# ScalarE instead of VectorE multiplies the GELU by the gate, and VectorE adds its own rows between two dot products

## The chip, the core and the metric

One core of a Trainium2 chip. The metric is the device time of one execution in microseconds. All numbers are float32. TensorE is called PE here, GpSimd POOL and ScalarE ACT where a row of the profile does so, and VectorE DVE.

## What is computed

Two layers of a trunk, over one block of 128 context tokens (block 0, group "P") and two blocks of 128 latent tokens (blocks 1 and 2, group "S"). Each layer is a token mixer (mLSTM, then attention) and behind it an expert lookup. It is the lookup that the change touches:

```python
def peer_ffn(h, w_q, subkeys, u, v):
    ...
    def one_block(xb):
        ...
        eidx = jnp.take_along_axis(cidx, pos, axis=-1)
        g = jax.nn.softmax(top, axis=-1).astype(xb.dtype)
        act = jax.nn.gelu(jnp.einsum('tped,td->tpe', u[eidx], xb), approximate=False)
        return jnp.einsum('tpe,tped->td', g * act, v[eidx])
```

For each token 8 heads choose 16 experts each, 128 in all. Of each expert a row of `u` (1024 numbers) is dotted with the token, the GELU of that is multiplied by the gate `g`, and the expert's row of `v` is added with this weight.

## The kernel before

**Groups.** There are 6 lookups (2 layers by 3 blocks), each of 128 slots, a slot being one expert for each of the 128 tokens. `u` and `v` lie side by side in memory, so one indirect DMA of POOL (L605) brings a slot: 128 rows of 8 KB, 1 MB. Two slots (GS = 2) are a group, so a lookup has 64 groups and the kernel 384. `rows` holds 12 slots, that is RING = 6 groups.

**The body of a group n on each engine.** VectorE waits for the two slots and makes two dot products (L1136, each with a short read of its accumulator), then raises `dots`. Then it does what is left of group n-1: `weigh` (L1120) multiplies the two GELU columns by two gate columns into `wv`, and raises `weighted`; and, for those groups whose ring place is in SIDE_PLACES (5 of 6 places in the lookups of block 0, 3 of 6 in the others), `add_up` (L1125) adds the second slot's `v` row with its weight into the tile `side`, 1024 columns wide. ScalarE waits for `dots`, makes the GELU of group n (all of ScalarE's activations are on L856) and then, when `weighted` of n-1 is there, the diagonal matrices of group n-1: a copy of the identity scaled by a column of `wv`, one for each slot that PE adds (one where there is a side sum, else two). PE, one group further behind, waits for the diagonals of n-2 and adds diagonal times `v` rows into the PSUM tile `acc` (L674; a diagonal costs two halves of 512 columns, which show as four matmul records). POOL gathers into a ring place anew when `summed` says that PE is done with the group six before, and `side_summed` that VectorE is.

**The order of the work.** `PLAN` is one list of steps for all engines. `spread` cuts the groups of a lookup into runs, ("GROUPS", layer, block, from, to), and puts them between the steps of the trunk by estimated costs; there are 178 runs, most of one or two groups. Every engine goes through the list in order; on ScalarE and VectorE some steps that wait for PE stand one run later (`in_order`). The last lookup has nothing beside it and is one run of 64 groups, a loop over registers. Steps that the text speaks of: PS (an expert choice's scores; VectorE copies them in L1388), PT, PC, PG (VectorE's top 16, ..., the gates; PG ends with the gate columns in L1446), NORM (ScalarE's square of x, VectorE's L1089 behind it), MLA to MLC (the mLSTM; the state product is in MLB, read by L1290), AS (attention scores, read by L1503), MOD (modulation from the weights in_ada_w) and FIN (L1520 adds `acc` and `side` when all 64 groups are summed). `dve_step` counts the steps that VectorE has finished.

**The functions of the change.** On ScalarE `group` and `last_groups`; on VectorE `weigh`, `add_up`, `group` and `last_groups`, which `run_groups` calls.

Of the kernel before, what the change touches and what calls it, by code (L numbers as in the profile page):

```python
# [15 lines left out]
ALU = mybir.AluOpType  # L16
ACT = mybir.ActivationFunctionType
AX = mybir.AxisListType

P = 128  # L20
# [12 lines left out]
SLOTS = PH * TOPK  # L33
GS = 2
GROUPS = SLOTS // GS
QUARTERS = 4
QH = PH // QUARTERS
RING = 6
# [8 lines left out]
BLOCKS = {"P": [0], "S": [1, 2]}  # L47
# [118 lines left out]
PLAN = list(plan())  # L166
# [124 lines left out]
def dve_ends(s):  # L291
    return s[0] in ("MLV", "MLG", "MLB", "MLN", "MLO", "OUT", "PT", "PC", "PG", "AN", "FIN", "YOUT", "NORM") \
        or (s[0] == "MOD" and s[2] in (1, 4))
# [27 lines left out]
def has_side(order, ring):  # L321

    return ring in SIDE_PLACES[order]
# [7 lines left out]
def trunk(nc, A, O):  # L331
    ctx = ExitStack()
    with ctx:
# [15 lines left out]
        gate = sb("gate", [P, 3, SLOTS])  # L349
        act_in = sb("act_in", [P, RING, GS])  # L350
        act_out = sb("act_out", [P, RING, GS])
        wv = sb("wv", [P, RING, GS])
# [34 lines left out]
        xn, at = area(0, D)  # L387
# [3 lines left out]
        cv, at = area(at, KC, 2 * P)  # L391
        va, at = area(at, 2, MH, DV + 1)
        Cst, at = area(at, MH, DV + 1)
# [12 lines left out]
        qkv, at = area(D, 2, QKV)  # L406
        qTa, at = area(at, AH // 2, 2 * P)
        kTa, at = area(at, AKV, 3 * P)
        kdup, at = area(at, AKV, 2, HD)
# [5 lines left out]
        qTp, at = area(D, NSETS, 2 * P)  # L415
        sc, at = area(at, NSETS, NKEYS)
        cand, at = area(at, PH // 2, TOPK * TOPK)
# [39 lines left out]
        act_step, dve_step = sem("act_step"), sem("dve_step")  # L457
# [8 lines left out]
        dots, gelus, weighted, diags, summed = sem("dots"), sem("gelus"), sem("weighted"), sem("diags"), sem("summed")  # L466
# [70 lines left out]

        GORDER = [(0, 0), (0, 1), (0, 2), (1, 0), (1, 1), (1, 2)]

        def run_groups(eng, s, body, last_ones):  # L540

            _, l, b, lo, hi = s
            order = GORDER.index((l, b))
            base = order * GROUPS

            def straight(g0, g1):  # L550
                for g in range(g0, g1):
                    n = base + g
                    body(order, n, g * GS, n % RING, n // RING, g)

            g = lo
            if g < 3:
                straight(g, min(3, hi))
                g = min(3, hi)
            whole = (hi - g) // RING
            if whole >= 2:  # L560
                with eng.Fori(0, whole) as i:
                    for k in range(RING):
                        n = base + g + k
                        body(order, i * RING + n, i * (RING * GS) + (g + k) * GS, n % RING, i + n // RING, None)
                g += whole * RING
            straight(g, hi)
            if hi == GROUPS:
                last_ones(order, base + GROUPS)
# [282 lines left out]
        def _(act):  # L851
# [3 lines left out]
            def f(out, in_, func, **kw):  # L855
                return nc.scalar.activation(out, in_, func, **kw)  # L856
# [13 lines left out]
            def diagonals(order, n, ring):  # L870

                act.wait_ge(weighted, n + 1)
                for j in range(GS - has_side(order, ring)):
                    last = f(diag[:, ring * GS + j, :], ident, ACT.Copy, scale=wv[:, ring, j:j + 1])
                last.then_inc(diags, 1)

            def group(order, n, slot, ring, turn, g):
                act.wait_ge(dots, n + 1)
                f(act_out[:, ring, :], act_in[:, ring, :], ACT.Gelu).then_inc(gelus, 1)
                if g != 0:  # L880
                    diagonals(order, n - 1, (ring - 1) % RING)

            def last_groups(order, n):
                diagonals(order, n - 1, (n - 1) % RING)
# [6 lines left out]
            for n_entry in in_order("A"):  # L891
                s = PLAN[n_entry]
# [11 lines left out]
                if dves:  # L904
                    act.wait_ge(dve_step, dves)
                if k == "GROUPS":
                    run_groups(act, s, group, last_groups)
                    continue
                if noted():
                    act.wait_ge(act_chain, noted())  # L910
# [10 lines left out]
                elif k == "NT":  # L921
                    _, l, w, b = s
# [3 lines left out]
                    place = tok(b - (b > 0))  # L926
                    for q in range(4):
                        last = f(hT[:, q, place], t[:, q * P:(q + 1) * P], ACT.Identity,
                                 scale=gain[:, l, w, q, c:c + 1], bias=modT[:, l, 24 * w + q, c:c + 1])
                    last.then_inc(act_freed, 1)  # L930
                elif k == "MLQK":
                    _, g, half = s
# [3 lines left out]
                elif k == "CONV":  # L936
                    _, g, half = s
# [141 lines left out]
        def _(dve):  # L1079
# [33 lines left out]
                        last.then_inc(dve_chain, one())  # L1113
                last.then_inc(dve_step, 1)

            def weigh(b, n, slot, ring):

                dve.wait_ge(gelus, n + 1)
                g = gate[:, b, slot:slot + GS] if isinstance(slot, int) else gate[:, b, bass.ds(slot, GS)]
                V.tensor_tensor(wv[:, ring, :], act_out[:, ring, :], g, ALU.mult).then_inc(weighted, 1)  # L1120

            def add_up(n, ring):

                dve.wait_ge(weighted, n + 1)
                V.scalar_tensor_tensor(side[:], rows[:, ring * GS + GS - 1, D:2 * D], wv[:, ring, GS - 1:GS], side[:],  # L1125
                                       ALU.mult, ALU.add).then_inc(side_summed, 1)

            def group(b, place):
                def body(order, n, slot, ring, turn, g):
                    if g == 0:  # L1130
                        V.memset(side[:], 0.0).then_inc(side_zero, 1)
                        dve.wait_ge(side_zero, n // GROUPS + 1)
                    for j in range(GS):
                        r = ring * GS + j
                        dve.wait_ge(rows_in[r], turn * 16 + 16)
                        last = V.tensor_tensor_reduce(out=rows[:, r, 0:D], in0=rows[:, r, 0:D], in1=xb[:, place, :],  # L1136
                                                      scale=1.0, scalar=0.0, op0=ALU.mult, op1=ALU.add,
                                                      accum_out=act_in[:, ring, j:j + 1])
                    last.then_inc(dots, 1)
                    if g != 0:  # L1140
                        weigh(b, n - 1, slot - GS, (ring - 1) % RING)
                        if has_side(order, (ring - 1) % RING):
                            add_up(n - 1, (ring - 1) % RING)
                return body

            def last_groups(b):
                def body(order, n):
                    weigh(b, n - 1, SLOTS - GS, (n - 1) % RING)
                    if has_side(order, (n - 1) % RING):
                        add_up(n - 1, (n - 1) % RING)  # L1150
                return body

            V.memset(cs[:], 0.0).then_inc(zeroed, 1)
            dve.wait_ge(inputs_in, 48)
            for n_entry in in_order("D"):
# [14 lines left out]
                if k == "GROUPS":  # L1170
                    if s[3] == 0:

                        dve.wait_ge(experts_chosen, QUARTERS * GORDER.index((s[1], s[2])) + 1)
                    run_groups(dve, s, group(s[2], GORDER.index((s[1], s[2])) % 2), last_groups(s[2]))
                    continue
                if noted():
                    dve.wait_ge(dve_chain, noted())
# [412 lines left out]
```

## Time and profile before

| what | us |
|---|---|
| median of 3 runs (2792.4 to 2797.18) | 2794.21 |
| span of the profiled execution, first to last instruction | 2786.9 |
| what lies around the span: median less span | 7.3 |
| PE busy (71%) | 1975.1 |
| VectorE busy (68%) | 1892.9 |
| POOL busy (31%) | 859.4 |
| ScalarE busy (21%) | 592.2 |
| gathers' packets, share of 16 DMA engines | 71.4% |
| packets of all other DMAs, the same | 17.2% |

The span is of one execution under the profiler; the profile gives no time of its own for that execution beside its span. Matmuls overlap and their ends are modelled. A row of the timeline has start, length, engine, line, operation, what is written from what, and in brackets the engine's idle time before it with who ended it. "x4" merges four instructions that follow each other.

### The profile page before, as it was taken

The numbers are of one execution on the slowest core, as the hardware profiler recorded it, in microseconds if no ns is written. First come the engines' busy times: TensorE is split into PE (matmuls) and PEld (weight loads), VectorE is DVE, ScalarE is ACT, GpSimd is POOL, SyncE is SP. The second block draws the span as 40 slices with busy tenths as digits, with TensorE's granted clock in tenths as the row PEclk, the third lists the DMA queues.
The fourth block names the chain that finished last, engine by engine and source line by source line (L and its number), as shares of the span: only waits on it lengthen the run. The fifth ranks groups of instructions, "written<-read, shape, count | busy, mean of one in ns | idle before, by whom it ended". The sixth has DMA issues, their size and how long they took to land. (4 is left out here: it accounts for less than half of the span.)

```text
span 2786.9 us, 22939 instructions
## 1 busy us (share of the span) xinstructions
PE 1975.1 (71%) x6742; PEld 1141.2 (41%) x6742; DVE 1892.9 (68%) x4473; ACT 592.2 (21%) x1595; POOL 859.4 (31%) x772
## 2 busy tenths in 40 slices
PE   6775686697777665677776775778868765767665
PEld 5465364365433222343443353445634322322222
DVE  1326885776877993256669765767778799866665
ACT  1211223332111211113212121232211121211111
POOL 0001322223333341123334423222343333444442
PEclk9787897799788887688888888677989877888888
DMA  9975797599898998899999988766999998899997
GB/s 340 308 200 226 290 363 289 219 355 356 355 376 362 382 390 315 305 362 395 352 358 415 412 319 336 277 245 246 381 371 408 367 402 362 361 391 422 422 422 293
DMA packets 259304, 958.06 MB, mean 344 GB/s; under 512 B 19700, under 2 KB 156916, under 8 KB 160884
## 3 DMA queue, kind: packets, MB, share of 16 engines
q0 software_dynamic: 110592, 805.36, 71.4%
q1 hardware_dynamic: 141296, 147.00, 16.6%
q10 hardware_dynamic: 7300, 4.33, 0.5%
q8 instruction: 52, 0.85, 0.1%
q14 instruction: 64, 0.52, 0.0%
HBM read 953.74 MB, written 2.89 MB: 343 GB/s over the span
## 5 line engine op out<-in xcount | busy, mean ns | idle before, releaser
L674 PE MATMUL acc<-rows,diag 128*128 128x512 f32 x2136 | 1182.8, 706 | 480.1 <-ACT diag L856 473.4
L605 POOL DMA_INDIRECT rows<-in_uv,eidx x768 | 859.2, 1119 | 1888.8 <-PE acc L674 1307.0
L1136 DVE CUSTOM_DVE_ANT_0 rows<-rows,xb 128x1024 f32<-128x1024 f32 x768 | 916.4, 1221 | 252.1 <-DMA rows<-in_uv,eidx 251.8
L674 PEld LDWEIGHTS acc<-rows,diag 128*128 128x128 f32 x2136 | 461.4, 226 | 1126.4 <-ACT diag L856 618.3
L856 ACT ACTIVATE act_out<-act_in 128x2 f32<-128x2 f32 x384 | 78.0, 203 | 1539.4 <-DVE act_in L1136 1538.8
L1125 DVE SCALAR_TENSOR_TENSOR side<-rows,wv,side 128x1024 f32<-128x1024 f32 x234 | 300.6, 1284 | 8.3
L623 PE MATMUL bank<-wt,hT 128*128 128x256 f32 x896 | 202.0, 386 | 11.4 <-ACT hT L856 7.4
L856 ACT ACT_TABLE_LOAD x137 | 175.8, 1283 | 138.8 <-DVE st L1089 36.7
L623 PE MATMUL bank<-hT,wt 128*128 128x256 f32 (+1 forms) x960 | 183.6, 353 | 17.9 <-DMA wt<-in_peer_w_q 12.6
L856 ACT ACTIVATE diag<-small,wv 128x128 f32<-128x128 f32 x534 | 192.0, 387 | 0.1
L623 PEld LDWEIGHTS bank<-wt,hT 128*128 128x128 f32 x896 | 173.2, 194 | 45.3 <-ACT hT L856 9.4
L623 PEld LDWEIGHTS bank<-hT,wt 128*128 128x128 f32 x960 | 164.3, 198 | 45.0 <-DMA wt<-in_peer_w_q 12.8
L623 PE MATMUL bank<-arena 128*128 128x64 f32 (+4 forms) x480 | 114.2, 429 | 14.3 <-DVE arena L1326 12.3
L623 PEld LDWEIGHTS bank<-arena 128*128 128x128 f32 (+1 forms) x480 | 95.1, 275 | 43.7 <-issue 17.7
L640 PE MATMUL bank<-small,arena 128*128 128x128 f32 x208 | 38.4, 340 | 81.2 <-DVE arena L1196 27.5
L1184 DVE TENSOR_TENSOR modT<-bank,small 128x4 f32<-128x4 f32 x48 | 7.3, 161 | 129.0 <-PE bank L623 128.9
L623 PE MATMUL bank<-wt,cs 128*32 128x256 f32 x432 | 37.1, 485 | 61.0 <-DMA wt<-in_ada_w 60.8
L1120 DVE TENSOR_TENSOR wv<-act_out,gate 128x2 f32<-128x2 f32 x384 | 60.2, 157 | 27.3 <-ACT act_out L856 27.3
L856 ACT ACTIVATE arena<-bank 128x256 f32<-128x256 f32 (+2 forms) x126 | 42.8, 372 | 152.4 <-PE bank L623 119.5
L640 PE MATMUL bank<-small,hT 128*128 128x128 f32 x160 | 37.9, 378 | 48.1 <-ACT hT L856 48.1
L640 PEld LDWEIGHTS bank<-small,arena 128*128 128x128 f32 x208 | 30.5, 175 | 96.6 <-issue 56.6
L1388 DVE COPY arena<-bank 128x512 f32<-128x512 f32 x24 | 16.5, 687 | 69.3 <-PE bank L623 68.8
(154 smaller groups left out, 1362.3 us busy)
## 6 DMA issues: line engine op xcount, KB each, us to landing
wt<-in_ada_w SPq DMA_DIRECT2D x27, 1024.0 KB
wt<-in_peer_w_q SPq DMA_DIRECT2D x26, 1024.0 KB
rows<-in_ada_w SPq DMA_DIRECT2D x21, 1024.0 KB, 12.0
wt<-in_mlstm_w_in SPq DMA_DIRECT2D x14, 1024.0 KB
rows<-in_uv,eidx POOLq DMA_INDIRECT x768
wt<-in_attn_w_qkv SPq DMA_DIRECT2D x12, 1024.0 KB
rows<-in_mlstm_w_in SPq DMA_DIRECT2D x10, 1024.0 KB, 12.1
wt<-in_attn_w_out SPq DMA_DIRECT2D x8, 1024.0 KB
```

Source lines behind the costliest of these rows:

```text
L605: nc.gpsimd.indirect_dma_start(out=rows[:, r, :], out_offset=None, in_=A["uv"], in_offset=bass.IndirectOffsetOnAxis(ap=eidx[:, b, slot:slo ...
L623: return nc.tensor.matmul(out, lhsT, rhs, start=start, stop=stop)
L640: last = nc.tensor.transpose(out[:, i * P:(i + 1) * P], a, ident)
L674: last = nc.tensor.matmul(acc[:, h * 512:(h + 1) * 512], diag[:, r, :], rows[:, r, D + h * 512:D + (h + 1) * 512], start=first and j == 0, ...
L856: return nc.scalar.activation(out, in_, func, **kw)
L1120: V.tensor_tensor(wv[:, ring, :], act_out[:, ring, :], g, ALU.mult).then_inc(weighted, 1)
L1125: V.scalar_tensor_tensor(side[:], rows[:, ring * GS + GS - 1, D:2 * D], wv[:, ring, GS - 1:GS], side[:], ALU.mult, ALU.add).then_inc(side_ ...
L1136: last = V.tensor_tensor_reduce(out=rows[:, r, 0:D], in0=rows[:, r, 0:D], in1=xb[:, place, :], scale=1.0, scalar=0.0, op0=ALU.mult, op1=AL ...
L1184: V.tensor_tensor(modT[:, l, n, :], t[:, 0:4].rearrange("p (n c) -> p n c", c=2), bc(ada_b[:, l, n], 2), ALU.add).then_inc(dve_freed, 1)
L1388: V.tensor_copy(sc[:, n, :], tile(0)[:].rearrange("p (e n) -> p e n", n=NKEYS)).then_inc(dve_freed, 1)
```

## The change

ScalarE waits for its own GELU and multiplies each of its two columns by the gate's column: two copies of one column each, scaled by a column of `gate`, written to `wv`. It raises `weighted` for group n itself, one body earlier than VectorE did, and goes on to the diagonals of n-1. Before each run it also waits until VectorE has made the gates that the run reads (`gates_after`). VectorE has no `weigh` any more. Its side sum of group n-1 stands behind the first of the two dot products of group n, and so ahead of the second; it waits there for `weighted` of n-1, and for its own `dots` of n-1. `dots` of n is raised behind the second dot product as before.

```diff
+        def gates_after(l, b, quarter):
+
+            g = "P" if b == 0 else "S"
+            at = PLAN.index(("PG", l, g, BLOCKS[g].index(b), quarter))
+            return sum(dve_ends(s) for s in PLAN[:at + 1])
...
-            def group(order, n, slot, ring, turn, g):
-                act.wait_ge(dots, n + 1)
-                f(act_out[:, ring, :], act_in[:, ring, :], ACT.Gelu).then_inc(gelus, 1)
-                if g != 0:
-                    diagonals(order, n - 1, (ring - 1) % RING)
+            def gate_at(b, slot):
+                return gate[:, b, slot:slot + 1] if isinstance(slot, int) else gate[:, b, bass.ds(slot, 1)]
+
+            def group(b):
+                def body(order, n, slot, ring, turn, g):
+                    act.wait_ge(dots, n + 1)
+                    f(act_out[:, ring, :], act_in[:, ring, :], ACT.Gelu).then_inc(gelus, 1)
+                    act.wait_ge(gelus, n + 1)
+                    for j in range(GS):
+                        last = f(wv[:, ring, j:j + 1], act_out[:, ring, j:j + 1], ACT.Copy, scale=gate_at(b, slot + j))
+                    last.then_inc(weighted, 1)
+                    if g != 0:
+                        diagonals(order, n - 1, (ring - 1) % RING)
+                return body
...
-                    run_groups(act, s, group, last_groups)
+                    act.wait_ge(dve_step, gates_after(*s[1:3], (s[4] - 1) * QUARTERS // GROUPS))
+                    run_groups(act, s, group(s[2]), last_groups)
...
-            def weigh(b, n, slot, ring):
-
-                dve.wait_ge(gelus, n + 1)
-                g = gate[:, b, slot:slot + GS] if isinstance(slot, int) else gate[:, b, bass.ds(slot, GS)]
-                V.tensor_tensor(wv[:, ring, :], act_out[:, ring, :], g, ALU.mult).then_inc(weighted, 1)
-
             def add_up(n, ring):
 
+                dve.wait_ge(dots, n + 1)
                 dve.wait_ge(weighted, n + 1)
                 V.scalar_tensor_tensor(side[:], rows[:, ring * GS + GS - 1, D:2 * D], wv[:, ring, GS - 1:GS], side[:],
                                        ALU.mult, ALU.add).then_inc(side_summed, 1)
...
                                                       accum_out=act_in[:, ring, j:j + 1])
+                        if g != 0 and j == 0 and has_side(order, (ring - 1) % RING):
+                            add_up(n - 1, (ring - 1) % RING)
                     last.then_inc(dots, 1)
-                    if g != 0:
-                        weigh(b, n - 1, slot - GS, (ring - 1) % RING)
-                        if has_side(order, (ring - 1) % RING):
-                            add_up(n - 1, (ring - 1) % RING)
                 return body
 
-            def last_groups(b):
-                def body(order, n):
-                    weigh(b, n - 1, SLOTS - GS, (n - 1) % RING)
-                    if has_side(order, (n - 1) % RING):
-                        add_up(n - 1, (n - 1) % RING)
-                return body
+            def last_groups(order, n):
+                if has_side(order, (n - 1) % RING):
+                    add_up(n - 1, (n - 1) % RING)
```

## Rows read from the trace of the kernel before

**Rows 1.** The page: busy time, share and instructions of each engine.

```profile
PE 1975.1 (71%) x6742; PEld 1141.2 (41%) x6742; DVE 1892.9 (68%) x4473; ACT 592.2 (21%) x1595; POOL 859.4 (31%) x772
```

**Rows 2.** Stretches: length, busy PE, PEld, DVE, ACT, POOL; clock, DMA share, GB/s.

```profile
2460.00:2760.00 300.00, 208.56 (x377) 83.31 (x376) 194.19 (x341) 42.24 (x157) 133.19 (x116) 0.84 1.00 415
910.00:1050.00 140.00, 86.48 (x183) 35.45 (x181) 134.35 (x401) 27.18 (x72) 53.46 (x48) 0.82 0.97 386
...
436.00:600.00 164.00, 114.19 (x357) 72.78 (x358) 123.81 (x238) 51.00 (x111) 41.09 (x36) 0.81 0.70 263
```

**Rows 3.** Who waited for whom over the span: us in total, times, longest.

```profile
POOL rows L605 <- PE acc L674: 1307.0, 212, 25.8
...
PE acc L674 <- ACT diag L856: 473.4, 154, 23.7
...
DVE rows L1136 <- DMA rows<-in_uv,eidx: 251.8, 162, 11.0
...
POOL rows L605 <- DVE side L1125: 69.1, 13, 15.3
DVE arena L1388 <- PE bank L623: 68.8, 13, 14.4
...
DVE wv L1120 <- ACT act_out L856: 27.3, 12, 14.7
```

**Rows 4.** Groups of instructions: busy us, mean ns, idle before and releaser.

```profile
L856 ACT ACTIVATE diag<-small,wv 128x128 f32<-128x128 f32 x534 | 192.0, 387 | 0.1
...
L856 ACT ACTIVATE act_out<-act_in 128x2 f32<-128x2 f32 x384 | 78.0, 203 | 1539.4 <-DVE act_in L1136 1538.8 <-issue 0.4
...
L1120 DVE TENSOR_TENSOR wv<-act_out,gate 128x2 f32<-128x2 f32 x384 | 60.2, 157 | 27.3 <-ACT act_out L856 27.3
...
L856 ACT ACTIVATE arena<-x 128x1024 f32<-128x1024 f32 x13 | 13.7, 1055 | 86.1 <-DVE x L1524 45.0 <-DVE x L1381 21.9 <-PE bank L623 15.2
```

**Rows 5.** Timeline of VectorE, two bodies between attention steps: start us, length us.

```profile
1868.42 1.22 DVE L1136 CUSTOM_DVE_ANT_0 rows<-rows,xb 128x1024 f32<-128x1024 f32 x1
...
1869.56 1.22 DVE L1136 CUSTOM_DVE_ANT_0 rows<-rows,xb 128x1024 f32<-128x1024 f32 x1
...
1870.71 0.15 DVE L1120 TENSOR_TENSOR wv<-act_out,gate 128x2 f32<-128x2 f32 x1
...
1870.90 1.28 DVE L1125 SCALAR_TENSOR_TENSOR side<-rows,wv,side 128x1024 f32<-128x1024 f32 x1
...
1872.10 1.22 DVE L1136 CUSTOM_DVE_ANT_0 rows<-rows,xb 128x1024 f32<-128x1024 f32 x1
...
1874.39 0.15 DVE L1120 TENSOR_TENSOR wv<-act_out,gate 128x2 f32<-128x2 f32 x1
1874.46 0.55 DVE L1503 TENSOR_REDUCE st<-bank 128x1 f32<-128x384 f32 x1
```

**Rows 6.** Timeline, the first run's end and a norm.

```profile
280.16 0.39 ACT L856 ACTIVATE diag<-small,wv 128x128 f32<-128x128 f32 x1
...
281.72 0.15 DVE L1089 TENSOR_SCALAR st<-st 128x1 f32<-128x1 f32 x1 [0.31 <-ACT xb L856]
```

**Rows 7.** Timeline: PE's links with diagonals ahead, and VectorE's wait for scores.

```profile
511.32 0.29 PEld L674 LDWEIGHTS acc<-rows,diag 128*128 128x128 f32 x1 [0.72 <-ACT diag L856]
...
1440.12 3.33 PE L674 MATMUL acc<-rows,diag 128*128 128x512 f32 x4 [4.10 <-ACT diag L856]
...
1457.11 0.69 DVE L1388 COPY arena<-bank 128x512 f32<-128x512 f32 x1 [4.09 <-PE bank L623]
```

**Rows 8.** Timeline of the last body and the end of the last lookup.

```profile
2767.54 0.20 ACT L856 ACTIVATE act_out<-act_in 128x2 f32<-128x2 f32 x1 [4.45 <-DVE act_in L1136]
2767.65 0.97 ACT L856 ACTIVATE diag<-small,wv 128x128 f32<-128x128 f32 x3
2767.77 0.16 DVE L1120 TENSOR_TENSOR wv<-act_out,gate 128x2 f32<-128x2 f32 x1 [0.20 <-ACT act_out L856]
...
2775.71 1.23 DVE L1520 TENSOR_TENSOR arena<-acc,side 128x1024 f32<-128x1024 f32 x1 [6.46 <-PE acc L674]
```

More of the change, by code:

```diff
@@ L1126, in add_up, with group @@
                                        ALU.mult, ALU.add).then_inc(side_summed, 1)
-            def group(b, place):
+            def group(place):
                 def body(order, n, slot, ring, turn, g):
@@ L1173, in _ @@
                         dve.wait_ge(experts_chosen, QUARTERS * GORDER.index((s[1], s[2])) + 1)
-                    run_groups(dve, s, group(s[2], GORDER.index((s[1], s[2])) % 2), last_groups(s[2]))
+                    run_groups(dve, s, group(GORDER.index((s[1], s[2])) % 2), last_groups)
                     continue
```

## The prediction

> **What bounds the kernel now.** I read the page's busy shares first [rows 1]: no engine is full (PE 71%, VectorE 68%), so no engine alone sets the span. Then the stretches [rows 2], where the reader is to see that the limit changes along the span. In the last block, 2460 to 2760, DMA is at 1.00 and 415 GB/s while VectorE has 194 of 300 us: a transfer bound. In 910 to 1050 VectorE is busy 134.35 of 140 us: a VectorE bound. In 436 to 600 DMA falls to 0.70 and no engine is full: there the trunk's steps and the gather groups take turns, and latency is the bound. So the change must be priced by stretch.
>
> The waits [rows 3] say which wait ends last. VectorE waits 251.8 us for rows. GpSimd waits 1307 us for PE's sums and only 69 us for side sums: a slot comes free when PE is done, and PE waits 473 us for the diagonals that ScalarE makes. VectorE itself waits for PE at the head of trunk steps, 13 times for scores (L1388, 68.8 us) and 6 times at the end of a block (L1520). What a faster VectorE gains ahead of such a wait is lost in it.
>
> **What VectorE sheds.** 384 products of 157 ns, 60 us in all [rows 4]. On the path each costs less or more, by its neighbours' starts [rows 5]. With a side sum: dot to dot 1.14, dot to product 1.15, product to side 0.19, side to dot 1.20, together 3.68 us (the row's columns are start and length); without the product 1.14+1.20+1.15 = 3.49, so 0.19 saved. Without a side sum the product costs the 0.07 between it and the next operation. A body of group n adds the side sum of n-1. Outside the last block I count 203 bodies with and 117 without: 38.6+8.2 = 46.8 us, the ceiling of the gain. In the last block, 31 and 33 bodies, the waits for rows cover it: nothing. Going back from the end along the waits, 77 bodies with and 42 without lie on the path outside it: 14.6+2.9 = **17.5 us saved**.
>
> **What the new order costs.** The sum of n-1 moves ahead of dot 1 of n. The dots of n, which release the GELU, the diagonals of n-1 and then PE, end 1.20 us later in a body with a side sum. The next body's start hardly moves. The side sum ends some 1.3 us earlier, but GpSimd's slot waits are PE's 19 to 1 [rows 3], so I give it nothing; the bounds are 0 and those 69 us, and I take 0, since a slot that opens early only helps where DMA has room.
>
> **What ScalarE takes on.** 768 copies and a wait for its own GELU. No one-column copy with a column scale is in the trace. Its duration: the diagonal of 128 columns takes 387 ns with such a scale; the square of 1024 takes 1055 and the GELU of two 203 [rows 4], thus 0.83 ns a column, and 387 less 106 is an estimated 281 ns. Three diagonals take 0.97 together [rows 8], 0.29 for each further one, so they overlap by 0.09 and copies follow at 0.19. The GELU starts the first diagonal 0.11 after its own start; a waiting product began 0.03 after its end [rows 8]. Afterwards: first copy at 0.20+0.03, diagonal at 0.23+0.19+0.19 = 0.61: **0.50 us later**. Bounds: copies at the GELU's spacing 0.11 give 0.34, at the diagonals' 0.29 give 0.70. I take 0.50, since its terms are from the same form.
>
> The Trainium skill (ScalarE: Activation LUTs, Rules for kernel authors) speaks against the move: multiplications belong on VectorE. By that rule the move is a loss on every group: the 157 ns given up for two copies of an estimated 279 ns each (What ACT_TABLE_LOAD costs: 186 and 93 for a pointer operand), which over 384 groups would be 154 us if ScalarE were the bound. The rows disagree as to the size: ScalarE is idle 1539 us before its GELUs [rows 4], so it has the room, and only the latency counts in my sum.
>
> ScalarE is in order, so behind the copies stand its diagonals and then the trunk step. Three rows show who is waiting.
> - A norm behind a body with a side sum [rows 6]: the diagonal starts at 280.16, the norm's square follows it at once, and VectorE waits 0.31 for that at 281.72. Afterwards the square is 1.20+0.50 = 1.70 later.
> - PE [rows 7]: the sum at 1440.12 waited 4.10 for a diagonal; behind it, with no idle time, come the queries' product, more sums and the scores, for which VectorE waits 4.09 at 1457.11. All of it moves by 1.70.
> - End of a block [rows 8]: diagonals at 2767.65, then PE's sums, for which VectorE idles 6.46. The last side sum isn't ahead of these dots: 0.50.
>
> Along the same path I find ScalarE's diagonals as a link in 9 places behind a body with a side sum and 22 without; 280.16 is the first and 2767.65 the last. One and two of them stand shortly before long waits for rows (up to 11.0 us [rows 3]) that take them in. 8 x 1.70 + 20 x 0.50 = **23.6 us lost**. Two runs of two groups ahead of a state product (448 and 508) become links: there PE already waited 0.72 for the second diagonal [rows 7], which now comes 1.70 later, less the 0.38 that two bodies save and some 0.2 of slack: 1.1 each, **2.2 lost**.
>
> **Edits that cost nothing.** The new wait of ScalarE for gates at each of 178 runs: VectorE makes those gates ahead of the dots for which ScalarE waits anyway; without that cover it would be 2.3 us of dots per run. VectorE's new wait for its weights stands before dot 1: queued behind are that dot and all later VectorE work. The weights are ready 0.04+0.61 us after the dots, the first dot of the next group takes 1.14, so it waits for nothing unless ScalarE is late. It was late for 27.3 us in all, 25 of it in the modulation steps [rows 3], where PE and ScalarE wait for the loads of in_ada_w: taking VectorE's stall away brings those no sooner. Registers for the gate's column are needed in the last block's loop alone, under the rows' waits. No DMA is added or moved in a queue.
>
> **Sum.** -17.5 + 23.6 + 2.2 = +8.3 us. The profiled execution has a span of 2786.9; the runs shown are 2792.4 to 2797.2, so some 7 us lie around the span. On the median of 2794.2 that makes **2802.5 us**.
>
> **Rivals.**
> - VectorE is the bound and the diagonals' delay is hidden. For it: 134 of 140 us in 910 to 1050, and PE's 6 us of slack in many choice steps. Against: the waits at L1388. Time: the 17.5 alone, 2777, at the very most 2747.5 by the ceiling; the case spans 2775 to 2788. It decides where fewer than about 10 diagonals are links. Chance 0.17.
> - A draw: transfers hold the pace. DMA is at 0.97 and 1.00 in two of the stretches [rows 2], and what shifts between such stretches is taken up by waits for rows. Both sums shrink to a third: 2797, or 2789 to 2799. Chance 0.30.
> - The slots starve: PE waits become slot waits. GpSimd waited 212 times for PE; were a quarter of these true links, 53 x 0.50 = 26 us would come on top: about 2829. Against it: where DMA is full, as in the last block, a slot that opens 0.5 later costs nothing. Chance 0.07.
> - The copies need a table load each time: 1283 ns. The diagonals are the same function and stand behind the GELU with no load [rows 8]; chance nearly nil.
> The forecast (2797 to 2815) has 0.46.
>
> **Numbers.** A measurement of this kernel tells about 0.2% (5.6 us) from no change. The forecast case is slower by that with 0.41 and within it with 0.05; the draw is within it with 0.26, else slower 0.03 and faster 0.01; the first rival faster with 0.16. Slower 0.51, same 0.32, faster 0.17. The range reaches from 2785, leaving out most of the first rival, to 2820, which is the forecast at 0.70 us a diagonal (+6) and some 10 us for links that the shift creates.
>
> **What would show it.** ScalarE busy up by 215 us, L1120 gone, copies near 0.28; gelu to diagonal 0.6; side sum between the dots, body 3.49; VectorE's waits at L1388, L1089 and L1520 longer, and longer PE waits for diagonals. It is wrong if VectorE's waits for PE and ScalarE stay and the choice stretches shrink, or if GpSimd's waits for PE grow by more than 50 us with lower DMA shares.

## The result, and the profile after

The changed kernel takes 2865.36 us (median; 2861.17 to 2868.22), the kernel before 2795.69 us beside it (2792.4 to 2801.11): a ratio of 1.0251, interval 1.0221 to 1.0281, so some 70 us slower. The forecast was 2802.5 with a range of 2785 to 2820; the sign was right, the size was outside the range. The profiled execution has a span of 2861.9 us, 75.0 more than the one before. In every run for which both are given, the time is 1.8 to 1.9 us above the run's own span. So the profiled execution of the kernel before took some 2789 us, about 5 us less than its median; the 7 us that were put "around the span" are mostly that.

Busy times of the kernel after, to be read against [rows 1]:

```profile
PE 1994.5 (70%) x6742; PEld 1150.0 (40%) x6742; DVE 1850.2 (65%) x4089; ACT 774.4 (27%) x2363; POOL 862.1 (30%) x772
```

The exchange of work is as announced: VectorE is busy 42.7 us less, ScalarE 182.2 us more (the pair of copies shows 0.48 us, since the two overlap). No engine became full. So the loss is in waits.

The same stretches of the kernel after as in [rows 2] (length, busy PE, PEld, DVE, ACT, POOL; clock, DMA share, GB/s):

```profile
2460.00:2760.00 300.00, 206.64 (x405) 86.19 (x404) 195.82 (x304) 79.67 (x284) 124.19 (x117) 0.84 0.99 409
910.00:1050.00 140.00, 88.40 (x179) 38.12 (x178) 130.93 (x372) 37.37 (x117) 57.61 (x48) 0.79 0.96 384
436.00:600.00 164.00, 104.23 (x320) 65.49 (x320) 109.15 (x203) 54.58 (x131) 35.87 (x33) 0.75 0.65 243
```

The stretches are by the clock on the wall, so they hold slightly other work than before; what counts is their kind. The transfer-bound one keeps its pace (0.99, 409 GB/s). The one bound by latency has DMA at 0.65 instead of 0.70, and VectorE and PE both do less in it.

Waits over the span of the kernel after (us in total, times, longest), against [rows 3]:

```profile
POOL rows L611 <- PE acc L680: 1428.5, 217, 26.3
ACT act_out L862 <- DVE act_in L1147: 1091.5, 279, 16.2
...
PE acc L680 <- ACT diag L862: 538.7, 147, 26.7
...
ACT L862 <- DVE act_in L1147: 378.6, 59, 16.4
DVE rows L1147 <- DMA rows<-in_uv,eidx: 258.1, 154, 12.9
...
DVE side L1136 <- ACT wv L862: 59.2, 41, 16.8
```

PE's waits for diagonals grew by 65.3 us and GpSimd's waits for PE by 121.5. The row that explains them has no tile's name: `ACT L862 <- DVE act_in`, 59 times. It is an instruction that names no tile and starts when the dots are done. The groups of instructions say which (busy us, mean ns, idle before and releasers):

```profile
L862 ACT ACT_TABLE_LOAD x137 | 175.8, 1283 | 474.0 <-DVE act_in L1147 378.6 <-DVE st L1105 32.9 <-DVE st L1511 22.7
L862 ACT ACTIVATE wv<-act_out,gate 128x1 f32<-128x1 f32 x768 | 184.2, 286 | 19.1
```

In the kernel before the same row reads:

```profile
L856 ACT ACT_TABLE_LOAD x137 | 175.8, 1283 | 138.8 <-DVE st L1089 36.7 <-DVE st L1277 23.9 <-DVE st L1505 19.4
```

There are as many table loads as before, 137, and each is as long, 1283 ns. They only stand elsewhere in time: 59 of them now come behind the dots. One of the 59, with 16.4 us, stands there before too, so 58 are new. The two timelines show one and the same place, an attention step followed by the body of group 221 (start, length, idle before and releaser). Before:

```profile
1836.98 1.28 ACT L856 ACT_TABLE_LOAD   x1
...
1844.20 3.23 PE L674 MATMUL acc<-rows,diag 128*128 128x512 f32 x4
...
1847.14 0.08 DVE L1136 DVE_READ_ACCUMULATOR2_ANT act_in<- 128x1 f32 x1
...
1847.26 0.20 ACT L856 ACTIVATE act_out<-act_in 128x2 f32<-128x2 f32 x1 [9.00 <-DVE act_in L1136]
...
1847.81 1.98 PE L674 MATMUL acc<-rows,diag 128*128 128x512 f32 x4 [0.38 <-ACT diag L856]
```

After:

```profile
1901.44 1.22 DVE L1147 CUSTOM_DVE_ANT_0 rows<-rows,xb 128x1024 f32<-128x1024 f32 x1
...
1902.58 1.28 DVE L1136 SCALAR_TENSOR_TENSOR side<-rows,wv,side 128x1024 f32<-128x1024 f32 x1
...
1903.78 1.22 DVE L1147 CUSTOM_DVE_ANT_0 rows<-rows,xb 128x1024 f32<-128x1024 f32 x1
...
1905.08 1.28 ACT L862 ACT_TABLE_LOAD   x1 [11.23 <-DVE act_in L1147]
...
1906.38 0.20 ACT L862 ACTIVATE act_out<-act_in 128x2 f32<-128x2 f32 x1
1906.61 0.48 ACT L862 ACTIVATE wv<-act_out,gate 128x1 f32<-128x1 f32 x2
1907.00 0.39 ACT L862 ACTIVATE diag<-small,wv 128x128 f32<-128x128 f32 x1
1907.20 1.28 DVE L1136 SCALAR_TENSOR_TENSOR side<-rows,wv,side 128x1024 f32<-128x1024 f32 x1 [1.05 <-ACT wv L862]
...
1907.44 1.55 PE L680 MATMUL acc<-rows,diag 128*128 128x512 f32 x2 [2.93 <-ACT diag L862]
```

Before, ScalarE loads the GELU's table right behind its last exponential at 1836.98 and then waits 9.00 us for the dots; the load is free. After, it sits idle for 11.23 us, until the dots are done, and only then loads, 1.28 us. The GELU, the copies, the diagonal, PE's sum and VectorE's next side sum, which waits 1.05 us, are all late by that. (PE's wait for the diagonal, 0.38 us before and 2.93 after, also holds the 1.20 us of the new order and the 0.50 us of the copies.)

Why it stands there is read in ScalarE's instructions at this place in order, with the semaphore that each waits for. Before:

```
L856 ACT_TABLE_LOAD
L856 ACTIVATE act_out<-act_in 128x2 [waits dots]
```

After:

```
L888 semaphore instruction [waits dots]
L862 ACT_TABLE_LOAD
L862 ACTIVATE act_out<-act_in 128x2 [waits dve_step]
```

The source puts the new wait for the gates (`dve_step`) ahead of the GELU's own wait for `dots`. With one wait, it rides on the GELU and the load ahead of it is free to run. With two, one becomes an instruction of its own, ahead of the load, and here it is `dots`, the one that ends last. Of the 62 loads ahead of a group's GELU, 59 stand behind such an instruction for `dots` after, and one before. Whether the two waits in the other order in the source would leave `dots` on the GELU was not tried.

### The profile page after: what moved, and what is told of

It reads as the page before. It is cut to its first block and busy times, and to the rows that moved or that the text cites. A ratio compares the mean times of both kernels' runs of the same rounds, so it can differ in the third digit from the quotient of the medians.

```text
span 2861.9 us, 23732 instructions
## 1 busy us (share of the span) xinstructions
PE 1994.5 (70%) x6742; PEld 1150.0 (40%) x6742; DVE 1850.2 (65%) x4089; ACT 774.4 (27%) x2363; POOL 862.1 (30%) x772
## 5 line engine op out<-in xcount | busy, mean ns | idle before, releaser
L680 PE MATMUL acc<-rows,diag 128*128 128x512 f32 x2136 | 1205.6, 718 | 552.3 <-ACT diag L862 538.7
L680 PEld LDWEIGHTS acc<-rows,diag 128*128 128x128 f32 x2136 | 469.4, 230 | 1205.6 <-ACT diag L862 674.3
L862 ACT ACTIVATE act_out<-act_in 128x2 f32<-128x2 f32 x384 | 78.0, 203 | 1093.7 <-DVE act_in L1147 1091.5
L1136 DVE SCALAR_TENSOR_TENSOR side<-rows,wv,side 128x1024 f32<-128x1024 f32 x234 | 300.2, 1283 | 59.2 <-ACT wv L862 59.2
L862 ACT ACT_TABLE_LOAD x137 | 175.8, 1283 | 474.0 <-DVE act_in L1147 378.6
L862 ACT ACTIVATE diag<-small,wv 128x128 f32<-128x128 f32 x534 | 191.4, 386 | 0.0
L862 ACT ACTIVATE wv<-act_out,gate 128x1 f32<-128x1 f32 x768 | 184.2, 286 | 19.1
L629 PE MATMUL bank<-hT,wt 128*128 128x256 f32 (+1 forms) x960 | 182.2, 352 | 6.0 <-ACT hT L862 6.0
L629 PE MATMUL bank<-arena 128*128 128x64 f32 (+4 forms) x480 | 112.9, 427 | 17.5 <-DVE arena L1332 13.6
L862 ACT ACTIVATE arena<-bank 128x256 f32<-128x256 f32 (+2 forms) x126 | 42.7, 370 | 153.5 <-PE bank L629 114.1
L646 PEld LDWEIGHTS bank<-small,arena 128*128 128x128 f32 x208 | 29.8, 172 | 97.3 <-issue 59.5
```

The source lines that it names most:

```text
L629: return nc.tensor.matmul(out, lhsT, rhs, start=start, stop=stop)
L646: last = nc.tensor.transpose(out[:, i * P:(i + 1) * P], a, ident)
L680: last = nc.tensor.matmul(acc[:, h * 512:(h + 1) * 512], diag[:, r, :], rows[:, r, D + h * 512:D + (h + 1) * 512], start=first and j == 0, ...
```

## The experiments

The theory tested, L: the second wait holds some 59 loads behind the dots, and this is most of the loss. Its rivals: O, the new order and the later diagonals starve the slots; C, the copies themselves load ScalarE too heavily. Every ratio below is to the kernel before, with five rounds; 1% is 28 us.

**The wait moved.** In the changed kernel:

```diff
-                    act.wait_ge(dve_step, gates_after(...))
...
                     f(act_out[:, ring, :], act_in[:, ring, :], ACT.Gelu).then_inc(gelus, 1)
+                    if g == first:
+                        act.wait_ge(dve_step, gates)
                     act.wait_ge(gelus, n + 1)
```

> The changed kernel, with ScalarE's new wait for the gates moved from ahead of a run of groups to behind the first GELU of the run, ahead of its two copies. Theory L (the load): with two waits ahead of the first GELU, the load of the GELU's table (1.28 us) comes behind the dots in 59 of 178 runs instead of beside them, and this is most of the loss. Then this kernel has the ACT_TABLE_LOAD waiting for dots at most a few times, its time falls by 50 to 65 us to about 2800 to 2815, and ScalarE's table loads wait about 139 us in all as in [rows 4]'s kernel. Theory O (the order): the side sum between the dots and the 0.5 us later diagonals cost it, starving the slots; the time stays at 2855 to 2865 and GpSimd's waits for PE stay at about 1430 us.

Measured: 1.0085 (1.0058 to 1.0111), 24 us above the kernel before, where the change has 70. The wait in its place cost 46 us (35 to 58 by the two intervals), somewhat under the expected 50 to 65. Its table loads:

```profile
L862 ACT ACT_TABLE_LOAD x137 | 175.8, 1283 | 114.1 <-DVE st L1107 29.6 <-DVE st L1285 20.3 <-DVE act_in L1149 16.4
```

16.4 us of waits for dots are left, one place, and that one the kernel before has too. GpSimd's waits for PE are at 1358.4 us, not at the 1430 of theory O. Rival C asked for 2850 us or more and falls here too: all 768 copies are in this kernel, and it is at 1.0085.

**The wait alone.** The kernel before, and nothing but this:

```diff
                 if k == "GROUPS":
+                    act.wait_ge(dve_step, gates_after(...))
                     run_groups(act, s, group, last_groups)
```

> The kernel before, with nothing changed but the wait of ScalarE for the gates ahead of each of its 178 runs of groups; the wait is redundant there, since VectorE does the product with the gate itself. Theory L: 59 or so table loads come behind the dots, 1.28 us each, up to 75 us; the time rises by 45 to 75 us to 2840 to 2870. Theory O: the wait is always met in time, so no change, 2795 within 6 us.

Measured: 1.0129 (1.0106 to 1.0152), 36 us slower by a wait that is always met in time. This is somewhat under the expected 45 to 75. The loads are behind the dots again:

```profile
L862 ACT ACT_TABLE_LOAD x137 | 175.8, 1283 | 465.8 <-DVE act_in L1143 342.8 <-DVE st L1096 35.7 <-DVE st L1512 27.3
```

Theory O has no place for this result.

**The wait kept, the load moved ahead of it.** In the changed kernel:

```diff
+                    f(spare[:], ident[:, 0:1], ACT.Gelu)
                     act.wait_ge(dve_step, gates_after(...))
```

> The changed kernel, both waits left ahead of each run's first GELU, but a one-column GELU of the identity into a spare tile put ahead of them: it waits for nothing of the run, so a table load can be made there, before the waits. Theory L (the wait costs only because it leaves the 1.28 us load behind the dots): as wait_behind_gelu, 2805 to 2825, with no table load that waits for dots. A rival W (a second wait ahead of the GELU is itself dear, for the semaphore or ScalarE's sequencer): it stays near 2850 to 2865.

Measured: 1.0075 (1.0051 to 1.0098), 21 us. Both waits stand where the change has them, 178 GELUs are added, and 49 us come back. No load waits for dots any more:

```profile
L863 ACT ACT_TABLE_LOAD x137 | 175.8, 1283 | 95.4 <-DVE st L1107 33.5 <-DVE st L1285 20.2 <-DVE st L1513 14.9
```

The wait as such is therefore not dear (rival W falls); what it does to the load is.

**The order alone.** The kernel before, with the product and the side sum of the group before placed between the two dots:

```diff
+                        if g != 0 and j == 0:
+                            weigh(b, n - 1, slot - GS, (ring - 1) % RING)
+                            if has_side(order, (ring - 1) % RING):
+                                add_up(n - 1, (ring - 1) % RING)
                     last.then_inc(dots, 1)
-                    if g != 0:
...
```

> The kernel before, with VectorE's product and side sum of the group before placed between the two dot products; ScalarE as it was. Theory L with the terms of the prediction: dots of a body with a side sum end 1.2 us later (and 0.2 for the product), 8 links of 1.4 us plus about 20 of 0.2, so 10 to 20 us slower, 2805 to 2815. Theory O: most of the 70 us appears, 2840 or more.

Measured: 1.0073 (1.0046 to 1.0101), 20 us: at the upper end of what L says, far from the 44 and more of O.

**The order taken back.**

```diff
-                        if g != 0 and j == 0 and has_side(order, (ring - 1) % RING):
-                            add_up(n - 1, (ring - 1) % RING)
                     last.then_inc(dots, 1)
+                    if g != 0 and has_side(order, (ring - 1) % RING):
+                        dve.wait_ge(dots, n + 1)
+                        add_up(n - 1, (ring - 1) % RING)
```

> As wait_behind_gelu, but with the side sum back behind both dot products, so that only the copies on ScalarE are left of the change. Theory L: 17.5 us saved on VectorE, 28 links of 0.5 us lost, about 2790 to 2800, 8 to 12 us below wait_behind_gelu. Theory O: near the kernel before as well if the order is what costs, but then 50 us or more below wait_behind_gelu. A third theory C (the copies themselves load ScalarE too heavily ahead of its diagonals): 2850 or more here and in wait_behind_gelu, and no change in the two kernels made from the kernel before.

Measured: 1.0048 (1.0029 to 1.0066), 13 us. Against wait_behind_gelu the order is worth 10 us (1 to 19 by the two intervals). It was to be near nothing against the kernel before, and isn't: either the copies cost more than 14 us or the dropped product brings less than 17.5. Two kernels tell these apart.

**The copies alone.**

```diff
                 f(act_out[:, ring, :], act_in[:, ring, :], ACT.Gelu).then_inc(gelus, 1)
+                act.wait_ge(gelus, n + 1)
+                for j in range(GS):
+                    f(spare[:, ring, j:j + 1], act_out[:, ring, j:j + 1], ACT.Copy, scale=act_in[:, ring, j:j + 1])
```

> The kernel before with the wait for the own GELU and two scaled one-column copies added behind it, into a spare tile; VectorE keeps its product and its order. It measures the delay alone. The prediction's term: the diagonals 0.5 us later at 28 links, +14 us, 2800 to 2810. If the change's saving on VectorE (17.5 us) is real, this kernel is some 17 us slower than wait_behind_old_order, about 2820 to 2825; if the saving is hidden, it equals it at about 2805.

Measured: 1.0052 (1.0032 to 1.0071), 14.5 us, the expected 14.

**The product alone taken away.**

```diff
-                V.tensor_tensor(wv[:, ring, :], act_out[:, ring, :], g, ALU.mult).then_inc(weighted, 1)
...
-                    last = f(diag[:, ring * GS + j, :], ident, ACT.Copy, scale=wv[:, ring, j:j + 1])
+                    last = f(diag[:, ring * GS + j, :], ident, ACT.Copy, scale=act_out[:, ring, j:j + 1])
```

> The kernel before without VectorE's product: the multiplication of GELU by the gate is left out of the computation, and the diagonals and the side sum take the GELU itself. It measures what the dropped product is worth. The prediction's term: 17.5 us faster. wait_behind_old_order (product dropped, copies added) and before_two_copies (copies added, product kept) stood at +0.48 and +0.52%, so by those two the saving is near nothing: 0 to 6 us faster.

Measured: 0.9977 (0.9961 to 0.9993), 6.4 us faster, 2 to 11 by the interval. The other pair that differs by the product, before_two_copies and wait_behind_old_order, is 1 us apart. Three rows of its trace:

```profile
PE 1977.6 (71%) x6742; PEld 1141.1 (41%) x6742; DVE 1863.1 (67%) x4089; ACT 591.6 (21%) x1595; POOL 869.6 (31%) x772
```

```profile
POOL rows L605 <- PE acc L674: 1317.0, 206, 25.8
...
DVE rows L1134 <- DMA rows<-in_uv,eidx: 283.1, 179, 11.3
```

VectorE is busy 29.8 us less than before and waits 31.3 us more for rows. GpSimd's wait for PE, which sets when rows are asked for, has hardly moved. That fits a VectorE that became free and waits for the same rows. It isn't shown: the execution in this trace is the longest of the 12 (a span of 2796.3 us, 9.4 above the one of the kernel before), and the same row in before_two_copies, which keeps the product, is 257.3 us, in wait_behind_old_order 268.6.

**The diagonals in their own body.** The kernel before has to make the diagonals of a group one body late, since VectorE makes the weights there. The change lifts this bond and doesn't use it. With the wait behind the GELU, and in the new order:

```diff
                     last.then_inc(weighted, 1)
-                    if g != 0:
-                        diagonals(order, n - 1, (ring - 1) % RING)
+                    diagonals(order, n, ring)
                 return body
...
             def last_groups(order, n):
-                diagonals(order, n - 1, (n - 1) % RING)
+                pass
```

> wait_behind_gelu with the three diagonals (two or one per group) of a group made in its own body, right behind its copies, instead of in the next body. In the kernel before they had to wait for VectorE's product of the next body; now ScalarE has the weights itself. Theory D (PE waits for diagonals only because they are made one body, often one run, too late): PE's waits for diagonals fall from 508 us to below 350, slots come free sooner, and the time falls below the kernel before, to 2700 to 2780. Rival: the sums' order and the slots hold the pace, PE then waits for the next group's diagonals as long; 2800 to 2815, as wait_behind_gelu.

Measured: 0.9802 (0.9774 to 0.9830), 55 us faster than the kernel before and 79 faster than wait_behind_gelu, from which it differs by this alone; the rival falls. PE's waits for diagonals fall to 376.8 us, less far than theory D's 350. Then the side sum was put back behind both dots, by the edit of wait_behind_old_order:

> own_body_new_order with the side sum back behind both dot products. If the order's cost (10 us between wait_behind_gelu and wait_behind_old_order) stands here too, 0.2 to 0.5% below own_body_new_order: ratio 0.975 to 0.978. If the side sum is now what frees the slots (GpSimd waits 200.7 us for it in own_body_new_order, against 69.1 in the kernel before), a later side sum costs: 0.980 to 0.985.

Measured: 0.9792 (0.9770 to 0.9814), median 2736.35 us, 58 us faster. The two own-body kernels can't be told apart by these intervals; the order's 10 us don't show here. Waits of own_body_old_order:

```profile
POOL rows L611 <- PE acc L680: 976.4, 161, 26.4
...
PE acc L680 <- ACT diag L862: 368.4, 112, 17.7
POOL rows L611 <- DVE side L1136: 367.9, 78, 19.0
```

PE waits 105 us less for diagonals than in [rows 3], and GpSimd 331 us less for PE. The side sum is now what frees many slots (367.9 us against 69.1 in [rows 3]), so the order's two effects, earlier side sums and later dots, may cancel; that was not tried further. The timeline of the same kernel at group 221, the place of the timelines above, shows what is gained:

```profile
1812.23 7.63 PE L680 MATMUL acc<-rows,diag 128*128 128x512 f32 x12
...
1815.29 0.20 ACT L862 ACTIVATE act_out<-act_in 128x2 f32<-128x2 f32 x1 [9.04 <-DVE act_in L1147]
...
1815.59 0.48 ACT L862 ACTIVATE wv<-act_out,gate 128x1 f32<-128x1 f32 x2
1816.10 0.40 ACT L862 ACTIVATE diag<-small,wv 128x128 f32<-128x128 f32 x1
```

PE does 12 matmuls of its sums in one go, 7.63 us, begun ahead of the GELU of the new run; the diagonals were there. There the changed kernel has 4 (at 1900.78) and then waits 2.93 us for a diagonal of the last run's group, and the kernel before has 4 and waits 0.38 us.

**PE's sums moved nearer, too.** In own_body_new_order, first by one body:

```diff
-                if g is None or g >= 2:
-                    add_up(order, n - 2, (ring - 2) % RING, g == 2)
+                if g is None or g >= 1:
+                    add_up(order, n - 1, (ring - 1) % RING, g == 1)
```

> own_body_new_order with PE's sums of a group one body behind its dots instead of two. If slots that come free earlier are worth anything where GpSimd waits for PE (1128.8 us), faster by a further 0.5 to 2%: ratio 0.96 to 0.975. If PE's waits for the next group's diagonals only take the place, unchanged at 0.980.

Measured: 0.9949 (0.9930 to 0.9968), 41 us slower than own_body_new_order. Then by two:

```diff
-                if g is None or g >= 2:
-                    add_up(order, n - 2, (ring - 2) % RING, g == 2)
+                add_up(order, n, ring, g == 0)
```

> own_body_new_order with PE's sums of a group in that group's own body. PE then waits at the end of each run for the last diagonals with trunk work queued behind. If that wait costs what freeing the slots gives, it is no better than own_body_sums_one_later or slower, 0.97 to 0.99; if slots decide, faster still, below 0.965.

Measured: 1.0682 (1.0653 to 1.0710), 246 us slower than own_body_new_order. Both expectations of a gain fail. PE's waits for diagonals, in these two kernels in turn (376.8 us in own_body_new_order):

```profile
PE acc L680 <- ACT diag L861: 491.3, 137, 17.7
```

```profile
PE acc L680 <- ACT diag L860: 755.0, 173, 17.7
```

PE is in order. A sum that waits for a diagonal holds the trunk's products behind it; the lag of two bodies is what keeps the diagonals ready. VectorE's waits for the scores (the line L1388 of [rows 3]) rise as the lag shrinks, from 58.5 us in own_body_new_order to 112.4 and 162.1, and GpSimd's waits for side sums from 200.7 to 285.6 and 647.8.

**The wait, once more.** own_body_new_order with the gates' wait left where the change has it, so against the change only the edit of the diagonals:

```diff
+                    act.wait_ge(dve_step, gates_after(...))
                     run_groups(act, s, group(s[2]), last_groups)
...
-                    if g == first:
-                        act.wait_ge(dve_step, gates)
```

> own_body_new_order with the gates' wait left where the change has it, ahead of each run's first GELU: the change with nothing altered but where the diagonals are made. Theory L: some 58 table loads stand behind the dots, 1.28 us each. If each delays the end as it does in the changed kernel, 36 to 46 us above own_body_new_order, 2780 to 2795. If the diagonals made a body earlier give slack that takes the load in (PE no longer waits for the diagonals of a run's first group), less than half of that: 2750 to 2770. PE's waits for diagonals would then stay near 377 us.

Measured: 0.9937 (0.9917 to 0.9958), so 38 us above own_body_new_order (28 to 48 by the two intervals): the full price, not half. PE's waits for diagonals are at 396.6 us, and the loads stand where L has them:

```profile
ACT L862 <- DVE act_in L1146: 381.3, 58, 16.4
```

It also says how large the missed chance was: even with the misplaced loads, the change with its diagonals moved, and nothing else, is 18 us faster than the kernel before.

## Why the prediction was wrong

**The step that failed** is the first of "Edits that cost nothing": the new wait of ScalarE for gates at each of 178 runs, covered because VectorE makes those gates ahead of the dots. That is true: no row of waits has ScalarE waiting for gates. But I asked only how long the wait lasts, and not what moves when a second wait stands ahead of an instruction with a hidden load. In its place the runs show 59 loads of 1.28 us, 75.7 us in all, behind the dots (one of them there already), of which 46 (change against wait_behind_gelu), 49 (against after_early_load), 36 (alone) and 38 us (with own bodies) reach the end. Each of these four differences is known to some 6 to 11 us. The term was 0. The price without that cover was also worked out on the wrong object, 2.3 us of dots per run.

The loads were in plain view: 137 of them, 175.8 us, on the engine that the change touches. The rival on table loads asked whether the copies need new ones; they don't, 137 it is. It did not ask when the old ones run. The Trainium skill (ScalarE: Activation LUTs, What ACT_TABLE_LOAD costs) gives about 1283 ns for a load, which all these traces agree with, and a drain of about 1380 ns on top, which they don't show: the GELU at 1906.38 starts 0.02 us after the load that began at 1905.08 has ended, and the load itself starts 0.08 us after the last dot at 1903.78 has ended.

By lookup the loss follows the loads only roughly. The first dot of the sixth lookup starts at 2534.8 us in the trace of the change and at 2488.9 in that of wait_behind_gelu. The table says in which lookup the 45.9 us between them arise (0.7 lie ahead of the first), and gives the same for before_with_wait against the kernel before, whose loads behind the dots are as many but for one fewer in the fifth:

| lookup | loads behind the dots in the change | change against wait_behind_gelu, us | before_with_wait against before, us |
|---|---|---|---|
| first | 20 | 10.5 | 10.9 |
| second | 7 | 10.8 | 6.2 |
| third | 10 | 0.6 | 2.3 |
| fourth | 14 | 19.1 | 10.3 |
| fifth | 8 | 4.3 | 7.9 |
| sixth | 0 | 1.5 | 0.3 |

The sixth row runs to the end of the span. The lookup without exposed loads loses next to nothing, in both pairs. Why the price of one differs so much, 0.06 to 1.5 us, was not separated. The 1.5 is more than a load takes, so single loads aren't all that these differences hold: each is between two single executions, and PE's granted clock differs between them too. That waits for rows take some loads in is likely, not shown.

**The other terms.** All but the wait was to be +8.3 us; wait_behind_gelu stands at +24 (16 to 31).
- VectorE's product: forecast 17.5 us, measured 6.4 (2 to 11). The direction was right, the size wrong by 11: I counted bodies along one chain of waits. Where the rest went isn't shown; longer waits for rows fit. This is the second step that failed, and it is the largest part of the 15 us between 8.3 and 24.
- The diagonals 0.50 us later: forecast 28 x 0.50 = 14 us, measured 14.5. GELU to diagonal is 0.62 in the timeline, forecast 0.61; a copy 286 ns, forecast 281.
- The order: forecast 8 x 1.20 and the better part of the 2.2, some 11 us; 10 between two kernels, 20 in the kernel before with the product moved as well.
- These three make -6.4 + 14.5 + 10.3 = 18.4 us, inside the interval of wait_behind_gelu. The 10.3 is itself a difference to wait_behind_gelu, so what this tests is that product and copies, 8.1 us, make up wait_behind_old_order, 13 (8 to 18): at the edge of its interval.
- The body without a product: from dot 1901.44 past side sum 1902.58 and dot 1903.78 to the next dot at 1904.92 it is 3.48 us, forecast 3.49.
- VectorE's new wait for its weights: it was to wait for nothing unless ScalarE is late. ScalarE is late wherever a load is exposed: 59.2 us in 41 waits, 27.2 with the loads hidden, and 27.3 at the old place in [rows 3].

The rivals: neither the VectorE bound nor the draw happened. "The slots starve" named the right symptom (GpSimd's waits for PE up by 121.5 us, above the 50 that I had set as a mark) but for the wrong reason: with the loads hidden these waits are up by 51.4 us, the other 70.1 go with the loads. At 2829 not even its price reached the result.

## What to carry to other kernels

A wait that is always met in time is not free if it is the second one ahead of an instruction that loads something first: look up on which instruction each wait lands, and whether a table load stands ahead of it. Put the new wait where its data are used, behind the first operation that needs the load. And when a step moves to another engine, look for the bonds it lifts: here the diagonals could be made in their own body. That took 79 us off wait_behind_gelu and left the kernel 55 us faster than before, while the product that was moved was worth 6.

## What the runs showed of the hardware that was not expected

- A table load takes no part in a wait that rides on the activation behind it, but stands behind a separate one: 16.4 us of waits for dots ahead of loads in the kernel before, at the one place where it too has more than one wait ahead of the GELU, 378.6 after.
- The slower kernels mostly show a lower granted clock of PE. Means over the span are 0.829 before, 0.819 after, 0.813 in before_with_wait and 0.836 in own_body_old_order. It isn't a matter of PE's idle time alone: that is 826 us in before_with_wait, and 834 in before_two_copies, whose clock is 0.829. Executions of the kernel before range from 0.820 to 0.835. PE's 2136 matmuls of the sums take 706 ns on average before, 1182.8 us in all, and after:

```profile
L680 PE MATMUL acc<-rows,diag 128*128 128x512 f32 x2136 | 1205.6, 718 | 552.3 <-ACT diag L862 538.7 <-issue 13.6
```

  That is 22.8 us of busy time more for the same sums. How much of it lies on the path, and so belongs to the 36 to 49 us of the loads, was not separated.
- Copies of one column with a column scale overlap: 286 ns each, 0.48 us for two, and the diagonal starts 0.39 us after the first of them.
